# The gate matrix of a sparse expert layer: one 256-column product a token instead of a 128-column f32 one, and its operands made on other engines

## The reference

```python
experts = e_a * PEER_N_KEYS + e_b
gw = jax.nn.softmax(sc, axis=-1)
...
u = u_tab[eb]
act = jax.nn.gelu(jnp.einsum('td,tkd->tk', xb, u).astype(jnp.float32), approximate=False)
wts = (gb * act).astype(v_tab.dtype)
return jnp.einsum('tk,tkd->td', wts, v_tab[eb])
```

## Time and profile before

| what | value |
|---|---|
| time, median of 3 runs | 1798.11 us (1797.17 to 1798.86) |
| the profiled execution | 1801.24 us, its span 1799.4 us |
| PE busy | 1747.2 us, 97% of the span |
| DVE, ACT, POOL busy | 70%, 52%, 27% |
| chain that ended last | PE 84%, of which 83% at the matmul helper L942; DVE 5%, ACT 4%, DMA 2%, POOL 2%, issue 2% |
| granted TensorE clock, mean | 0.991 |
| early units | from about 621 to 770 us of the span |
| gated units | from about 777 to 1014 us |
| late units | from about 1018 to 1049 us |

### The profile page before, as it was taken

One profiled execution on the slowest core, in us unless ns is written; L12 is line 12 of the kernel. 1 busy time (PEld: TensorE's weight loads), 2 busy tenths in 40 slices (PEclk: granted clock), 3 DMA queues, 4 the chain that ended last, 5 costly groups with the idle time before them and its releaser, 6 DMA issues.

```text
span 1799.4 us, 33010 instructions
## 1 busy us (share of the span) xinstructions
PE 1747.2 (97%) x11190; PEld 1550.6 (86%) x11190; DVE 1252.0 (70%) x2359; ACT 940.7 (52%) x1389; POOL 489.8 (27%) x225
## 2 busy tenths in 40 slices
PE   9999999999999999999999999999999999989997
PEld 6899878897878999999999988888888677669996
DVE  4667577776424499067777578888888896667777
ACT  5476576544555544567777543333333575334444
POOL 4156734401568588800000000000000000003332
PEclk9999989999999999999999999999999999999999
DMA  6644443577344477765555687777677783355553
GB/s 216 222 176 141 167 139 118 193 246 264 121 164 150 135 226 224 231 177 175 174 174 174 191 263 235 238 238 236 234 237 238 275 267 114 115 177 186 182 183 114
DMA packets 122839, 347.63 MB, mean 193 GB/s; under 512 B 13904, under 2 KB 46800, under 8 KB 122512
## 3 DMA queue, kind: packets, MB, share of 16 engines
q1 hardware_dynamic: 121248, 339.52, 57.8%
q0 software_dynamic: 1520, 7.21, 1.1%
HBM read 328.84 MB, written 17.83 MB: 193 GB/s over the span
## 4 chain that ended last, share of the span: by engine, by line
PE 84%; DVE 5%; ACT 4%; DMA 2%; POOL 2%; issue 2%; POOLq 0%; SPq 0%; ACTq 0%; DVEq 0%
PE banks L942 83%; DMA weight_ring<-in_stream 2%; POOL weight_rest L858 2%; ACT arena L1684 2%; ACT weight_high L1684 1%; PE banks L953 1%; DVE weight_rest L2316 1%; ACT span_exponentials L1684 0%; DVE arena L3119 0%; DVE arena L3000 0%; ACT L1684 0%; ACT scratch L1684 0%; DVE arena L2357 0%; DVE arena L2354 0%; DVE arena L2494 0%
## 5 line engine op out<-in xcount | busy, mean ns | idle before, releaser
L1684 ACT ACTIVATE weight_high<-weight_ring 128x1024 fp32r<-128x1024 f32 x448 | 471.9, 1055 | 453.3 <-PE banks L942 351.1
L858 POOL TENSOR_TENSOR weight_rest<-weight_ring,weight_high 128x1024 fp32r<-128x1024 f32 (+1 forms) x165 | 411.7, 2504 | 268.2 <-ACT weight_high L1684 154.1
L2316 DVE TENSOR_TENSOR weight_rest<-weight_ring,weight_high 128x1024 fp32r<-128x1024 f32 x283 | 346.1, 1224 | 159.6 <-ACT weight_high L1684 156.3
L942 PE MATMUL banks<-a_high,weight_high 128*128 128x256 f32 x1216 | 304.0, 288 | 0.2 <-ACT weight_high L1684 0.2
L942 PE MATMUL banks<-a_rest,weight_high 128*128 128x256 f32 x1216 | 297.8, 283 | 0.0
L942 PEld LDWEIGHTS banks<-a_high,weight_high 128*128 128x128 f32 x1216 | 232.5, 191 | 1.6 <-issue 1.1
L942 PEld LDWEIGHTS banks<-a_rest,weight_high 128*128 128x128 f32 x1216 | 232.9, 192 | 0.3 <-issue 0.2
L942 PE MATMUL banks<-weight_high,gated_high 128*128 128x512 f32 x512 | 201.4, 393 | 0.0
L942 PE MATMUL banks<-weight_high,gated_rest 128*128 128x512 f32 x512 | 200.2, 391 | 0.0
L942 PE MATMUL banks<-a_high,weight_rest 128*128 128x256 f32 x1216 | 170.9, 283 | 2.4 <-POOL weight_rest L858 2.4
L942 PE MATMUL banks<-x_high,weight_high 128*128 128x256 f32 x672 | 167.5, 287 | 4.7 <-DVE x_rest L3088 3.7
(11 more groups left out here) (360 smaller groups left out, 3109.3 us busy)
## 6 DMA issues: line engine op xcount, KB each, us to landing
weight_ring<-in_stream SPq DMA_DIRECT2D x512, 512.0 KB, 3.5
arena<-in_stream SPq DMA_DIRECT2D x66, 512.0 KB, 3.3
unit_spill<-small SPq DMA_DIRECT2D x128, 128.0 KB, 3.6
scratch<-unit_spill SPq DMA_DIRECT2D x128, 128.0 KB, 3.2
residual<-in_x SPq DMA_DIRECT2D x2, 512.0 KB, 4.2
arena<-in_mem POOLq DMA_DIRECT2D x2, 512.0 KB, 5.2
arena<-in_ctx POOLq DMA_DIRECT2D x2, 512.0 KB, 4.4
arena<-in_keys POOLq DMA_DIRECT2D x1, 1024.0 KB, 5.1
```

The lines of the kernel that those rows point to most:

```text
L858: nc.gpsimd.tensor_tensor(used_columns(e, w_lo[:, e % 2, :]), used_columns(e, raw(e)[0]), used_columns(e, w_hi[:, e % 2, :]), ALU.subtract ...
L942: return nc.tensor.matmul(out, lhsT, rhs, start=start, stop=stop, skip_group_check=True)
L1684: return nc.scalar.activation(out, in_, f, **kw)
L2316: tt(w_lo[:, e % 2, :], raw(e)[0], w_hi[:, e % 2, :], ALU.subtract).then_inc(S[ready], 1)
```

## The change

The gate of each pick is split into a rounded high part and a rest (new rows 2 and 3 of `expert_slots`). For each token the row one-hots come in two forms side by side, times the high part and times the rest, in the one-pass number form; the column one-hots are written in that form too. So one one-pass product of 128 by 256 columns a token replaces the f32 product of 128 columns, and the two halves are added when the result leaves PSUM.

- PE: four matmuls of 256 columns a quad. A quad's result takes banks 6 and 7 together, so there is one buffer for it. PE also waits for the copies of `eTr` before `cH`.
- DVE: two instructions make a quad's rows (`row_onehots`), and a sum over the two halves, from PSUM into `WT`, takes the place of ACT's copy (`dense`). It makes no unit rests any more.
- ACT: makes all columns. For u = 0 and 2 four squares and a Relu; for u = 1 and 3 one square of differences that POOL has written, and a Relu.
- POOL: makes the rests of all units, the gated and the late ones too, and the differences for u = 1 and 3 (`column_distances`).
- The late units use banks 4 and 5 alone, and SP waits for the last gate product before it loads the first units back.

```diff
-UD = U0 + 52
+UD = U0 + P
...
-    B.loop("w", T // 16, 4, banks=(6, 7, 6, 7))
-    B.loop("u3", U_LATE // 4, 4, banks=(4, 5, 6, 7))
+    B.loop("w", T // 16, 4, banks=(6, 6, 6, 6))
+    B.loop("u3", U_LATE // 4, 4, banks=(4, 5, 4, 5))
...
+        columns_r = over("column_onehots_one_pass", "column_onehots", 0, [P, 2, 4, P])
+        rowhots = over("row_onehots", "scratch", 0, [P, 2, 4, 2, P])
+        gates_high = over("gates_high", "scratch", 0, [P, T])
...
+        GATE_SUMS = ps[:, 6:8, :].rearrange("p b (v x n) -> p (b v) x n", v=2, x=2)
...
+            def column_distances(u, turn=None):
+                i_ = 0 if turn is None else turn
+                b, n = B.at[("w", u)]
+                pool.wait_ge(bank_full[b], i_ * 4 + (n - 2))
+                quad = bc(slots[:, 1, bass.ds(i_ * 16 + 4 * u, 4)], 2, P)
+                nc.gpsimd.tensor_tensor(column_onehots[:, 1], bc(C("iota"), 1, 4), quad,
+                                        ALU.subtract).then_inc(S["pool_columns"], 1)
...
+            with pool.Fori(1, T // 16) as i:
+                for j in range(4):
+                    if j % 2:
+                        column_distances(j, i)
+                    split_rest(U0 + U_EARLY + j, i, 4)
+            with pool.Fori(0, U_LATE // 4) as i:
+                for j in range(4):
+                    split_rest(U0 + U_EARLY + U_GATED + j, i, 4)
...
+            for t in range(TT):
+                freed(pe, ("eTr", t))
             pe.wait_ge(S["ctx_kd"], 1)
...
                     pe.wait_ge(S["onehot_ready"], i * 4 + (u + 1))
-                    if u == 0:
-                        pe.wait_ge(S["column_ready"], i + 1)
-                    else:
-                        pe.wait_ge(S["dve_columns"], i * 3 + u)
-                    b = claim(("w", u), i)
+                    pe.wait_ge(S["column_ready"], i * 4 + (u + 1))
+                    claim(("w", u), i)
                     for v in range(4):
-                        ins = mm(b[:, hsl(v)], COLUMN[:, u % 2, v, :], ROWHOT[:, u % 2, v, :])
+                        ins = mm(GATE_SUMS[:, v], columns_r[:, u % 2, v, :], rowhots[:, u % 2, v])
...
+            def columns(token, u, made):
+                if u % 2 == 0:
+                    for v in range(4):
+                        ins = func(column_onehots[:, 0, v, :], C("iota"), ACT.Square, scale=-1.0,
+                                   bias=slots[:, 1, bass.ds(token + v, 1)])
+                else:
+                    act.wait_ge(S["pool_columns"], made)
+                    ins = func(column_onehots[:, 1], column_onehots[:, 1], ACT.Square)
                 ins.then_inc(S["square_made"], 1)
...
+                func(columns_r[:, u % 2], column_onehots[:, u % 2], ACT.Relu, scale=-1.0, bias=1.0).then_inc(S["column_ready"], 1)
...
                 split_high(U0 + U_EARLY + u + 2, i, 4)
-                dense(i, u)
+                if more:
+                    arrived(act, ("w", u), i)
+                    columns(i * 16 + (4 * u + 8), u, i * 2 + (u // 2 + 2))
...
+            step(cp(gates_high[:, :], slots[:, 2, :]))
+            step(tt(slots[:, 3, :], slots[:, 2, :], gates_high[:, :], ALU.subtract))
...
+            def row_onehots(token, u, count):
+                rests = rowhots[:, u % 2, :, 1, :]
+                tt(rests, bc(C("iota"), 1, 4), bc(slots[:, 0, bass.ds(token, 4)], 2, P), ALU.is_equal).then_inc(step.c.sem, 1)
+                dve.wait_ge(step.c.sem, made + count)
+                gates_ = bc(slots[:, 2:4, bass.ds(token, 4)].rearrange("p x v -> p v x"), 3, P)
+                tt(rowhots[:, u % 2], bc(rests, 2, 2), gates_, ALU.mult).then_inc(S["onehot_ready"], 1)
+
+            def dense(turn, u):
+                arrived(dve, ("w", u), turn)
+                out = WT[:, :, bass.ds(turn * 16 + 4 * u, 4)].rearrange("p n v -> p v n")
+                free(V.tensor_reduce(out, GATE_SUMS.rearrange("p v x n -> p v n x"), AX.X, ALU.add), ("w", u))
...
+            with dve.Fori(0, T // 16 - 1) as i:
                 for u in range(4):
-                    split_rest(UD + u, "lo_ready", i, 4)
...
+                    dense(i, u)
+                    row_onehots(i * 16 + (4 * u + 8), u, i * 4 + (u + 3))
```

More of the change, by code:

```diff
@@ L897, in _ @@
                     split_rest(U0 + j, i, 4)
+            def column_distances(u, turn=None):
[5 more added lines that the diff above has]
+                                        ALU.subtract).then_inc(S["pool_columns"], 1)
+            split_rest(U0 + U_EARLY)
+            for t in range(TT):
+                freed(pool, ("eTr", t))
+            for j in range(1, 4):
+                if j % 2:
+                    column_distances(j)
+                split_rest(U0 + U_EARLY + j)
+            with pool.Fori(1, T // 16) as i:
+                for j in range(4):
+                    if j % 2:
+                        column_distances(j, i)
[3 more added lines that the diff above has]
+                    split_rest(U0 + U_EARLY + U_GATED + j, i, 4)
             for s in range(4):
@@ L2062, in _, with unit_and_columns @@
                 evacuate(("cH", d), h0[:, d], src=quarters)
[L2064 to L2069, removed]
-                ins.then_inc(S["square_made"], 1)
[L2071 to L2080, removed]
+            for t in range(TT):
+                freed(act, ("eTr", t))
+            def columns(token, u, made):
[3 more added lines that the diff above has]
+                                   bias=slots[:, 1, bass.ds(token + v, 1)])
+                else:
+                    act.wait_ge(S["pool_columns"], made)
+                    ins = func(column_onehots[:, 1], column_onehots[:, 1], ACT.Square)
+                ins.then_inc(S["square_made"], 1)
+                act.wait_ge(S["square_made"], (2 * made - 1) if u % 2 == 0 else 2 * made)
+                func(columns_r[:, u % 2], column_onehots[:, u % 2], ACT.Relu, scale=-1.0, bias=1.0).then_inc(S["column_ready"], 1)
+            columns(0, 0, 1)
+            columns(4, 1, 1)
+            def unit_and_columns(i, u, more=True):
                 act.wait_ge(h_out[u], i * 16 + 16 * U_EARLY // 4)
@@ L2797, in _ @@
-            with dve.Fori(0, U_LATE // 4) as i:
-                for j in range(4):
-                    split_rest(UD + U_GATED + j, "lo_ready", i, 4)
+            step(cp(gates_high[:, :], slots[:, 2, :]))
+            step(tt(slots[:, 3, :], slots[:, 2, :], gates_high[:, :], ALU.subtract))
+            made = step.c.n
+            def row_onehots(token, u, count):
[4 more added lines that the diff above has]
+                tt(rowhots[:, u % 2], bc(rests, 2, 2), gates_, ALU.mult).then_inc(S["onehot_ready"], 1)
@@ L2801, in _ @@
+            for u in range(4):
+                dense(T // 16 - 1, u)
+                if u < 2:
+                    row_onehots(T - 8 + 4 * u, u, T // 4 - 1 + u)
+            step.c.n = made + T // 4
             for u in range(4):
```

27 lines of the change are left out of this document (7 added, 20 removed).

## The result

The changed kernel takes 1870.76 us (median of 4 runs, 1869.03 to 1874.99) against 1798.48 us for the kernel before in the same runs: a ratio of 1.0398, 95% interval 1.0383 to 1.0414. It is slower by 72 us; 1886 was forecast, in a range of 1838 to 1925. The profiled execution took 1872.49 us with a span of 1870.6 us.

The account below looks back on a forecast made before the run. It took PE as the bound before, and turns of DVE and POOL at the shared SBUF access after: +85.8 for 64 steps and +1.7 at the edge, +87.5 us, 1888.7 from the profiled execution, stated as 1886; range 1838 to 1925.

Parts of the forecast that it names:

- The mechanism: Gated stretch: DVE's row instructions and POOL's rests and differences, all with two SBUF operands, take turns; +1.34 us a step.
- the prediction's rival without contention: Gated stretch: repeated-element operands leave POOL alone, PE decides at 3.35 us a step; -24.5 us, 1774; chance 0.05.
- Its condition: DVE beside POOL: with at most one SBUF operand on DVE neither side notices; with two, both wait.
- The step: Gated stretch: 5.1 us a step, between 4.86 and 5.25, against 3.76 before; 64 steps give +85.8 us.
- The layout by hand: Gated stretch: one pair of quads laid out event by event, 10.5 us a pair, 5.25 a step.
- the accident: Gated stretch: high part 0.4 us later, forms precede the second rest; pairs of 8.3 and 11.15, mean 9.7.
- PE idle before the products: Gated stretch: PE idles 3.8 of 10.5 us a pair, ended by DVE, once a pair much longer.
- a floor of 4.39: Gated stretch: shared-access time of rests, differences, ones and forms, 8.78 us a pair, 4.39 a step, not reached.
- The edges: Before the gated stretch: PE waits for ACT's copies of the transposes, 1.7 us; gate splitting and late units at nothing.
- Shared access alone: Gated stretch: POOL or DVE always has work for the access; 4.39 us a step, 1840; chance 0.12.
- Both sums in the chain: Gated stretch: both sums of a pair stand in the chain with their products; 6.26 us a step, 1960; chance 0.06.
- The clock: Gated stretch: PE idling in short pieces brings half clock; 6.7 us a step throughout, +190, 1988; chance 0.05.

Follow-up runs that it names:

- Without the turns the same program: Changed kernel with the iota and one quad's gates in PSUM, so both DVE row instructions read one operand there: 1776.03 us.
- the half-sum run: Changed kernel, but DVE copies only the half with the high parts of the gates out of the banks instead of adding both halves: 1855.62 us.
- the useless work on PE: Changed kernel with eight useless matmuls of 256 columns into bank 3 ahead of each gate product: 1883.87 us.
- without the differences: Changed kernel with no column differences on POOL, ACT making every quad's columns from four squares and a Relu: 1849.32 us.

## Why the prediction was right

- **The mechanism** (a row instruction with two SBUF operands and POOL's instructions, in turns) was right, and it is the whole of the loss; only DVE's side was varied, POOL's instructions read two operands from SBUF in every run. Without the turns the same program takes 1776, where the prediction's rival without contention came to 1774. PE's own step, 3.35 by the sum, is 3.34.
- **Its condition** was read too widely. The prediction has it that a DVE instruction with at most one operand from SBUF goes unnoticed; the sums that it names do. But in the same early stretch a TENSOR_SCALAR, which has one tensor operand, was recorded with 1.85 and ended 0.08 after a rest, and the next of the same shape took 0.21:

```profile
704.20 2.40 POOL L858 TENSOR_TENSOR weight_rest<-weight_ring,weight_high 128x1024 fp32r<-128x1024 f32 x1 [0.42 <-ACT weight_high L1684]
704.83 1.85 DVE L2733 TENSOR_SCALAR arena<-arena 128x128 uint32<-128x128 uint32 x1
706.60 0.21 DVE L2734 TENSOR_SCALAR arena<-arena 128x128 uint32<-128x128 uint32 x1
```

  The third of the three operations after 118 us is such a one too (L2459, 2.32); in all, the eleven TENSOR_SCALARs from SBUF to SBUF of that trace that met a rest with 0.3 us or more left ended behind it. For this change nothing hangs on it, since both its row instructions have two.
- **Own durations.** Ones 0.68, forms 1.22, sum 1.22 and differences 1.04 in the undisturbed kernels, against 0.68, 1.23, 1.22 and 1.1 taken. The choice of 1.22 for the sum instead of the 2.2 of its upper bound held; the copy of the half-sum run (1.05) suggests that the exchange does cost time when every element read is also written.
- **The step**, taken at 5.1, is 4.83 in the stretch (4.87 with the last sums). The mis-sized term is this +1.34, which measured +1.07 to +1.11. The layout by hand had 10.5 us a pair, and the pair shown above is that layout, event by event, in 10.25 (867.96 to 878.21). But it is the rarer one: from sum to sum of the even quads, quads 8 to 58 (DVE's timeline), there are four pairs of 10.25, ten of 8.25 to 8.28, and eleven of 10.92 to 11.78. The last two kinds follow each other by turns; they are what the prediction called the accident, worked out as 8.3 and 11.15, mean 9.7 (4.86). Both layouts were right, and 5.1 gave too much weight to the first. It is the one at full clock (10.27 a pair with the useless work on PE), but here pieces of half clock make ACT's high part late enough for the forms to go first. The prediction weighed the clock only as slower work of PE, not as something that moves the high part; by the run with the useless work this is why the time came out below the forecast.
- **PE idle before the products** was forecast with 3.8 us a pair and a long wait once a pair. It is 61 us in 304, 1.9 a pair, and the longest of the waits comes mostly once in two pairs, as the layouts alternate. A part of the idle time is filled by matmuls at half clock: PE is busy for 242.9 us where 63 steps of 3.34 are 210.
- **What bounds it.** The prediction spoke of the shared access with a floor of 4.39 and of chains on top. The simpler reading, shown by six kernels with waits, is that DVE has hardly a gap: a step is DVE's own time (3.1 us in the change) plus what its instructions wait. The floor decides nothing: without the differences it falls to 3.84 and the step stays at 4.44.
- **The edges**, 1.7, measured 2.5 at the start: 1.6 is PE's wait, as worked out, and some 0.6 is ACT's first gated gelu, which starts at 777.67, when ACT has made the columns of two quads, and not when PE is done. The 3.9 at the end were not in the sum. The last product waits 2.51 for a sum behind the last forms (recorded with 3.30), and after that wait unit 116 runs at a mean granted clock of 0.62, 1.6 us longer: the one place where the clock was seen to cost time.
- **The rivals.** Shared access alone: its 1840 was passed by 31 us. Both sums in the chain: no, a step takes 4.83 on average and not 6.26. The clock: half clock was granted for 58 of 304 us, less than the third that the prediction called hidden, and with the clock held full the step was longer, 5.08. The late stretch is unchanged (31.7 us, PE busy throughout).
- **The account.** Against the profiled execution, 87.5 were forecast and 71.2 measured: the steps with the end came out 14.5 lower (71.3 against 85.8), the start 0.8 higher, and 2.6 lie in stages that the change does not touch.

## What to carry to other kernels

Before moving elementwise work to GpSimd, count on VectorE the instructions that will then run beside it with two SBUF operands: each waits for what is left of the GpSimd instruction it meets, and a VectorE with slack by its own durations can become the bound. Look first for a second operand that can lie in PSUM; here that made 1871 into 1775. A scalar in place of a tensor is no way out by itself: the TENSOR_SCALAR of 704.83 us waited. Read the wait as an instruction recorded too long against the same one undisturbed, since the views show it as busy time.

## What was not expected of the hardware

A copy of 512 elements a partition out of PSUM, with the order exchanged, takes 1.05 us on DVE, nearly the 1.22 of a sum of 1024 that writes the same 512; the plain 512-element sum took 0.69. A form with a scalar, one PSUM and one SBUF operand of 256 elements is recorded with 0.48 and four follow each other in 1.65. In the pair shown the turns go by who asks first, with leads of 0.4 us and, for the forms of 868.71, 0.25 us, and the wait is recorded as the waiting instruction's own time: POOL's rests are recorded with 2.76 on average after, 2.93 without the differences, and 2.41 undisturbed.
